# States kept at every second token, one scan for all tiles, and a decay product in four column quarters, in a two-block fp32 kernel

## The chip, the cores and the metric

The kernel runs on one core of a Trainium2 chip. The metric is the time of one execution on the device in microseconds (us). The engines are TensorE (PE; its weight loads are shown as PEld), VectorE (DVE), ScalarE (ACT), GpSimd (POOL) and SyncE (SP), which issues the loads of the weights.

## The reference

Two transformer-like blocks run one after the other on 256 tokens of width 2048, all in float32. The first has an attention, a gated linear attention (GLA) and a short convolution, the second has an attention with a window and an S5 state space, and each has a feed-forward part. Two places of it matter here.

The decay of the GLA goes through a product of rank 16:

```
z = (a_down @ gla_w_up[l]) + gla_b[l]          # a_down: 16 columns of h @ w_in
log_a = jax.nn.log_sigmoid(z) / GLA_GATE_TAU
```

The state space has 32 groups of 16 inputs and 64 complex states. Its states follow x[t] = A x[t-1] + B u[t], with A diagonal and complex, and its output is y = C x + D u:

```
bu_re = jnp.einsum('gph,blgh->blgp', bb_re, ug)
bu_im = jnp.einsum('gph,blgh->blgp', bb_im, ug)
...
_, _, xs_re, xs_im = lax.associative_scan(combine, (a_re_t, a_im_t, bu_re, bu_im), axis=1)
y = (jnp.einsum('ghp,blgp->blgh', c_re, xs_re)
     - jnp.einsum('ghp,blgp->blgh', c_im, xs_im)
     + d_skip.reshape(SSM_GROUPS, SSM_GROUP) * ug)
```

The output goes through an exact GELU and a gated linear unit (`w_glu`) into the second branch of the block.

## The kernel before

**Panels.** Every large product is cut into panels of 512 output columns for both tiles of 128 tokens. The weights come in chunks of four 128-row blocks, and each chunk is used in two pieces of two blocks (one or two blocks in the last chunks of the down projections). For each piece ScalarE writes the weights rounded to fp32r (`weights_hi`, L1202), VectorE writes the rest (`weights_lo`, L1772), and TensorE does three products for each row block and token tile: hi by hi (L584), lo by hi (L585), hi by lo (L586). A piece of two row blocks so has 12 panel matmuls. ScalarE and VectorE split three pieces ahead (`AHEAD = 3`), in a ring of four.

**Side work.** All else is written as generators, one of the same name for each engine. After each piece the engine's program takes one turn of its generator (`side.step()`), up to its next `yield`; in the panels of `q2` every fourth piece takes a second turn. A generator's end takes a turn as well. `side.finish()` runs what is left. Each engine works in its own program order; the engines meet at semaphores. Side work of TensorE (transposes at L608, products at other lines) thus stands between panel matmuls, and writes four PSUM banks called `side`. fp32 products appear in the trace as two records for each matmul call, transposes as one.

**The decay.** `a_down` splits `w_a_down` (16 columns) into hi and lo and multiplies it in three products for each of 16 row blocks, four row blocks to a turn (L761 to L763, 12 matmuls). Later `gla` multiplies the result by `w_up` (L842, 16 rows).

**The state space.** The states stand in 16 tiles of 128 (two groups each). `ssm_setup` runs beside the first panel of `down1`: VectorE works out A, the scaled B (`bb_re`, `bb_im`) and powers of A, TensorE transposes B. The matrices B and C have 32 rows or columns for each tile. After panel `u2`, `ssm_first_half` transposes u, and `ssm_input(0)` forms B u for the first eight tiles at all 256 tokens: for each tile one product of the real and one of the imaginary part in the row group of that tile (32 rows; L955, L956), four tiles to a turn. ScalarE copies them to `ssm_states` (L1552). `scan(0)` on GpSimd then goes over them: the 256 tokens are 16 blocks of 16; 15 steps inside all blocks at once, 15 carries from block to block, and then corrections of the tokens in each block by powers of A times the block's carry (L466, L468), three tiles at a time for six tiles. The other two tiles of the half are corrected by VectorE in `scan_end` (L2303, L2305), whose turns lie in those of the third of the attention's eight head pairs. `ssm_halves` follows them: `ssm_output(0)` multiplies by C (L973, L974: four tiles in four column quarters, two tiles' groups of `u` to the half), `ssm_input(1)` forms the second half, and `scan(1)` runs. Its output, `ssm_output(1)` in `ssm_end`, is taken beside the third panel of `branch_attn`, with VectorE's `scan_end(1)` beside the first two. The second half stands in the same memory as the first, so that it can't be formed before the first is used.

The waits at the place:

```
        pe.wait_ge(ev["scanned"], half + 1)
        pe.wait_ge(ev["scanned_dve"], half + 1)
        pe.wait_ge(ev["cT"], 2)
```

## Time and profile before

| | |
|---|---|
| median of 3 runs | 2915.58 us (2915.02 to 2915.74) |
| the profiled execution | 2915.55 us |
| its span, first to last instruction | 2914.3 us |
| TensorE's mean granted clock over the span | 0.997 of full |
| busy: PE, DVE, ACT, POOL | 2887.7, 1659.2, 1325.9, 284.7 us |
| data read from HBM | 532.55 MB, 183 GB/s over the span |

A row of the timeline has the start, the duration (of the merged run of instructions), engine, line, operation, output tile and inputs, shapes and count, and in brackets how long the engine was idle before it and what ended that. The drawn duration of a matmul is longer than the distance to the next one, since matmuls are pipelined: the distance between starts is what they cost. A wait is put down to the semaphore that came last.

### The profile page before, as it was taken

The page shows a single profiled execution, that of the slowest core. Times are in us where ns is not written, and L with a number is a line of the kernel's source. Part 1 is how long each engine was busy: PE and PEld are TensorE (multiplying, and loading weights), DVE is VectorE, ACT ScalarE, POOL GpSimd, SP SyncE. Part 2 cuts the span into 40 slices and gives each one's busy share as a digit, 9 for nine tenths or more (in the row PEclk, how much of TensorE's full clock was granted, in tenths as well). Part 3 has the DMA queues.
Part 4 walks back from the last instruction along what each step waited for, and adds up shares of the span by engine and source line. Part 5 has one row for each costly group of instructions (what it writes and reads, how often), then busy time and mean ns, then how long its engine had stood idle before and what let it go on. Part 6 is the DMA issues. An engine that isn't in the chain of part 4 may idle for free.

```text
span 2914.3 us, 32236 instructions
## 1 busy us (share of the span) xinstructions
PE 2887.7 (99%) x13280; PEld 2376.8 (82%) x13280; DVE 1659.2 (57%) x1874; ACT 1325.9 (45%) x1635; POOL 284.7 (10%) x369
## 2 busy tenths in 40 slices
PE   9999999999999999999999999999999999999998
PEld 7888887788888888888888888787788888888887
DVE  5464655555555554554574557667755666656444
ACT  5444445444444444444444455444544444444443
POOL 0000000000000000000000049795100000000000
PEclk9999999999999999999999999999999999999999
DMA  7545454555655566555655656454655555555563
GB/s 250 196 165 194 158 187 144 171 190 188 194 188 183 186 192 195 188 190 188 199 187 183 200 166 206 151 171 138 198 186 188 187 184 192 173 196 188 194 201 131
DMA packets 279295, 536.74 MB, mean 184 GB/s; under 512 B 17313, under 2 KB 20317, under 8 KB 279149
## 3 DMA queue, kind: packets, MB, share of 16 engines
q1 hardware_dynamic: 267520, 528.52, 55.4%
q10 hardware_dynamic: 11629, 6.17, 0.8%
q8 instruction: 105, 1.72, 0.2%
q14 instruction: 41, 0.34, 0.0%
HBM read 532.55 MB, written 2.10 MB: 183 GB/s over the span
## 4 chain that ended last, share of the span: by engine, by line
PE 93%; POOL 4%; DVE 1%; ACT 1%; issue 1%; DMA 0%; ACTq 0%; DVEq 0%; POOLq 0%
PE panels L584 30%; PE panels L586 29%; PE panels L585 29%; PE side L608 2%; POOL scan_step L442 1%; POOL ssm_states L447 1%; POOL scan_step L439 1%; POOL ssm_states L446 1%; POOL ssm_states L468 1%; POOL ssm_scratch L466 1%; DVE weights_lo L1772 0%; PE side L896 0%; PE side L597 0%; PE side L892 0%; PE side L881 0%
## 5 line engine op out<-in xcount | busy, mean ns | idle before, releaser
L1772 DVE TENSOR_TENSOR weights_lo<-weights,weights_hi 128x1024 fp32r<-128x1024 f32 (+1 forms) x1032 | 1258.2, 1225 | 1040.0 <-ACT weights_hi L1202 1034.6
L1202 ACT ACTIVATE weights_hi<-weights 128x1024 fp32r<-128x1024 f32 (+1 forms) x1032 | 1064.8, 1036 | 1140.0 <-PE panels L586 1121.9
L584 PE MATMUL panels<-weights_hi,xT_hi 128*128 128x512 f32 (+1 forms) x2752 | 1085.2, 394 | 0.9 <-DVE xT_lo L1820 0.8
L586 PE MATMUL panels<-weights_hi,xT_lo 128*128 128x512 f32 (+1 forms) x2752 | 1070.0, 389 | 0.0
L585 PE MATMUL panels<-weights_lo,xT_hi 128*128 128x512 f32 (+1 forms) x2752 | 1068.5, 388 | 0.0
L584 PEld LDWEIGHTS panels<-weights_hi,xT_hi 128*128 128x128 f32 x2752 | 517.4, 188 | 110.3 <-issue 7.4
L586 PEld LDWEIGHTS panels<-weights_hi,xT_lo 128*128 128x128 f32 x2752 | 516.9, 188 | 108.8
L585 PEld LDWEIGHTS panels<-weights_lo,xT_hi 128*128 128x128 f32 x2752 | 517.8, 188 | 101.7
L584 PE MATMUL panels<-weights_hi,hiddenT_hi 128*128 128x512 f32 x704 | 275.2, 391 | 0.0
L586 PE MATMUL panels<-weights_hi,hiddenT_lo 128*128 128x512 f32 x704 | 274.1, 389 | 0.0
L585 PE MATMUL panels<-weights_lo,hiddenT_hi 128*128 128x512 f32 x704 | 274.0, 389 | 0.0
L586 PEld LDWEIGHTS panels<-weights_hi,hiddenT_lo 128*128 128x128 f32 x704 | 132.1, 188 | 27.7
L585 PEld LDWEIGHTS panels<-weights_lo,hiddenT_hi 128*128 128x128 f32 x704 | 132.2, 188 | 27.3
L584 PEld LDWEIGHTS panels<-weights_hi,hiddenT_hi 128*128 128x128 f32 x704 | 132.2, 188 | 26.9
L398 POOL TENSOR_TENSOR rstd<-mean_squares,minus_half 128x2 f32<-128x2 f32 x5 | 3.5, 699 | 1286.5 <-DVE mean_squares L1835 1286.5
L398 POOL TENSOR_TENSOR rstd_first<-mean_squares,minus_half 128x2 f32<-128x2 f32 x1 | 0.7, 690 | 736.0 <-DVE mean_squares L1835 736.0
L442 POOL TENSOR_TENSOR scan_step<-ssm_states,ssm_vectors 128x128 f32<-128x128 f32 (+1 forms) x120 | 64.3, 559 | 0.0
L447 POOL TENSOR_TENSOR ssm_states<-ssm_states,scan_step 128x256 f32<-128x256 f32 (+1 forms) x60 | 52.0, 866 | 4.7
L584 PE MATMUL panels<-weights_hi,merged2T_hi 128*128 128x512 f32 x128 | 50.8, 397 | 0.0
L381 POOL TENSOR_TENSOR rstd_gla<-mean_squares,minus_half 128x2 f32<-128x2 f32 x4 | 2.8, 692 | 490.9 <-DVE mean_squares L2148 490.9
L584 PE MATMUL panels<-weights_hi,mixedT_hi 128*128 128x512 f32 x128 | 50.6, 395 | 0.0
L586 PE MATMUL panels<-weights_hi,merged2T_lo 128*128 128x512 f32 x128 | 50.0, 390 | 0.0
(323 smaller groups left out, 2090.4 us busy)
## 6 DMA issues: line engine op xcount, KB each, us to landing
weights<-in_w_in SPq DMA_DIRECT2D x162, 1024.0 KB, 5.0
weights<-in_w_up SPq DMA_DIRECT2D x88, 1024.0 KB, 5.0
weights<-in_w_ffn_gate SPq DMA_DIRECT2D x44, 1024.0 KB, 5.2
weights<-in_w_ffn_up SPq DMA_DIRECT2D x44, 1024.0 KB, 5.2
weights<-in_w_out SPq DMA_DIRECT2D x32, 1024.0 KB, 5.3
weights<-in_w_ffn_down SPq DMA_DIRECT2D x32, 1024.0 KB, 5.1
weights<-in_w_down SPq DMA_DIRECT2D x32, 1024.0 KB, 5.1
weights<-in_w_ffn_down SPq DMA_DIRECT2D x16, 768.0 KB, 4.4
```

Source lines behind the costliest of these rows:

```text
L439: pool.tensor_tensor(same, prev, row(0, 2), ALU.mult).then_inc(ev["pool_step"])
L442: pool.tensor_tensor(cross[:, c:c + 1], prev[:, 1 - c:2 - c], row(2 + c, 1), ALU.mult).then_inc(ev["pool_step"])
L446: step(pool.tensor_tensor(cur, cur, same, ALU.add))
L447: return pool.tensor_tensor(cur, cur, cross, ALU.add)
L466: step(pool.tensor_tensor(tmp, pr, last, ALU.mult))
L468: inst = pool.tensor_tensor(cur, cur, tmp, op)
L584: pe.matmul(acc, a, wh, start=k0 + k == 0, stop=False)
L585: pe.matmul(acc, a, wl, start=False, stop=False)
L586: inst = pe.matmul(acc, b, wh, start=False, stop=k0 + k == total - 1)
L608: return self.pe.transpose(out, in_, self.m.IDENT[0:in_.shape[0], 0:in_.shape[0]])
L1202: self.act.activation(self.m.HI[:, g % PIECES, 0:n], raw, ACT.Copy).then_inc(self.ev["hi_split"])
L1772: self.dve.tensor_tensor(m.LO[:, ring, 0:n], raw, m.HI[:, ring, 0:n].bitcast(F32), ALU.subtract).then_inc(self.ev["lo_split"])
```

## The change

The scan keeps only the state at the odd token of each pair. `ssm_input` forms AB u[2k] + B u[2k+1] in PSUM, for two state tiles to a bank, from two products with a moving operand that takes every second token, all 16 tiles at once right after `u2`. The scan works with A squared over 128 pairs: blocks of 8 pairs, 7 steps in two halves of the tiles that follow each other with scratch of their own, 15 carries over all tiles, corrections four tiles at a time. GpSimd does all of it, and VectorE's `scan_end` is gone. `ssm_output` (four turns behind the attention, in the last gate panel) takes the odd tokens as C x, and the even tokens as CA x[previous odd] + CB u[even], where CB (32x32 for each tile) and CA are made beforehand: CB by TensorE in `ssm_setup`, CA by VectorE in `ssm_input`. C is loaded and transposed in `ssm_setup` rather than after `u2`. The GELU follows in the same stage as the output.

In the decay, `w_a_down` stays fp32, padded with zeros to 32 columns, and each of four column quarters takes one of four row blocks, so that the result stands in four partial sums of 32 rows; `w_up` stands four times among zero rows and adds them up in the product with 128 rows.

Not in the cut below: names, memory offsets (`XS` holds 16 tiles of 128 pairs; `gate_bias_rows` moves), GpSimd's memset of `w_a_down` and VectorE's of `w_up`, four issues of the load of `w_up` instead of one, the coefficient rows that now hold A squared, VectorE's six products for CA, ScalarE's copies of CB and C, and the turns of ScalarE's GELU.

```diff
-    def scan(self, half):
+    def scan(self):
...
-        X5 = XS[:, :, :, :].rearrange("p c s (b j) -> p c s b j", j=BLK)
-        pool.wait_ge(ev["states_in"], nt * (half + 1))
+        X5 = m.XS[:, :, :, :].rearrange("p c s (b j) -> p c s b j", j=BLK2)
+        pool.wait_ge(ev["states_in"], nt)
...
             step(pool.tensor_tensor(cur, cur, same, ALU.add))
-            return pool.tensor_tensor(cur, cur, cross, ALU.add)
-
-        for j in range(BLK - 1):
-            step(advance(X5[:, :, :, :, j], X5[:, :, :, :, j + 1], 20, NB))
+            step(pool.tensor_tensor(cur, cur, cross, ALU.add))
+
+        for j in range(BLK2 - 1):
+            for half in range(2):
+                tiles = slice(half * nt, (half + 1) * nt)
+                advance(X5[:, :, tiles, :, j], X5[:, :, tiles, :, j + 1], m.STEP[:, half], 20, tiles, NB)
         for b in range(NB - 1):
-            inst = advance(X5[:, :, :, b:b + 1, BLK - 1], X5[:, :, :, b + 1:b + 2, BLK - 1], 24, 1)
-            if b < NB - 2:
-                step(inst)
-        inst.then_inc(ev["carried"])
-        pool.wait_ge(ev["carried"], half + 1)
-
-        nb, nj, ns = NB - 1, BLK - 1, 3
+            advance(X5[:, :, :, b:b + 1, BLK2 - 1], X5[:, :, :, b + 1:b + 2, BLK2 - 1], m.CARRY, 24, slice(0, ST), 1)
+
+        nb, nj, ns = NB - 1, BLK2 - 1, 4
         tmp = m.SCR[:, 0:ns * nb * nj].rearrange("p (s b j) -> p s b j", b=nb, j=nj)
-        for q in range(0, nt - SHARED, ns):
+        for q in range(0, ST, ns):
             for ci in range(2):
                 cur = X5[:, ci, q:q + ns, 1:NB, 0:nj]
                 for y in range(2):
-                    pr = m.POW[:, (ci + y) % 2, s0 + q:s0 + q + ns, 0:nj].unsqueeze(2).to_broadcast([P, ns, nb, nj])
-                    last = X5[:, y, q:q + ns, 0:nb, BLK - 1:BLK].to_broadcast([P, ns, nb, nj])
+                    pr = m.POW[:, (ci + y) % 2, q:q + ns, 1:2 * nj:2].unsqueeze(2).to_broadcast([P, ns, nb, nj])
+                    last = X5[:, y, q:q + ns, 0:nb, BLK2 - 1:BLK2].to_broadcast([P, ns, nb, nj])
                     step(pool.tensor_tensor(tmp, pr, last, ALU.mult))
                     op = ALU.subtract if (ci, y) == (0, 1) else ALU.add
                     inst = pool.tensor_tensor(cur, cur, tmp, op)
-                    if q + ns == nt - SHARED and (ci, y) == (1, 1):
+                    if q + ns == ST and (ci, y) == (1, 1):
                         inst.then_inc(ev["scanned"])
                     else:
                         step(inst)
...
 
         self.panel(plan.u2, X, side)
-        side.add(self.ssm_first_half(), self.ssm_outputs_setup())
+        side.add(self.ssm_input(), self.pause(3))
         for pan in plan.q2:
             self.panel(pan, X, side, dense=True)
         self.panel(plan.kv2, X, side)
-        side.add(self.attention2())
+        side.add(self.attention2(), self.ssm_output())
         for pan in plan.gate_attn + plan.gate_ssm:
             self.panel(pan, X, side)
         side.finish()
         pe.wait_ge(ev.attention[1]["outT_lo"], HEADS2 // 2)
         for p in range(3):
-            if p == 2:
-                side.add(self.ssm_end())
             self.panel(plan.branch_attn[p], (m.OH2, m.OL2), side)
         side.finish()
+        pe.wait_ge(ev["gel_lo"], 2)
         for pan in plan.glu:
             self.panel(pan, (m.GEH, m.GEL), side)
         side.add(self.glu_turned())
...
         yield
-        pe.wait_ge(ev["wad_lo"], 1)
-        ps = self.bank(0)[0:RANK, 0:S]
-        for k in range(KD):
-            pe.matmul(ps, m.WADH[:, k, :], m.XH[:, k, :], start=k == 0, stop=False)
-            pe.matmul(ps, m.WADL[:, k, :], m.XH[:, k, :], start=False, stop=False)
-            inst = pe.matmul(ps, m.WADH[:, k, :], m.XL[:, k, :], start=False, stop=k == KD - 1)
-            if k % 4 == 3 and k < KD - 1:
+        pe.wait_ge(ev["loaded_decay"], 16)
+        ps = self.bank(0)
+        for first in range(0, KD, 4):
+            for x in (m.XH, m.XL):
+                for g in range(4):
+                    k = first + g
+                    inst = pe.matmul(ps[32 * g:32 * g + 32, 0:S], m.WAD[:, k, :], x[:, k, :].bitcast(F32),
+                                     start=first == 0 and x is m.XH, stop=k >= KD - 4 and x is m.XL)
+            if first < KD - 4:
                 yield
...
+        pe.wait_ge(ev["bb_ready"], 4)
+        for b, src in enumerate((m.ABR, m.ABI)):
+            ps = self.bank(2 + b)
+            for u in range(4):
...
+            self.free(i, "cT", i + 1)
+        yield
+        pe.wait_ge(ev["cT"], 2)
+        ps = self.bank(0)
+        for u in range(4):
+            for bb, ct in ((m.BBR, m.CTR), (m.BBI, m.CTI)):
+                for j in range(4):
+                    s = 4 * u + j
+                    inst = pe.matmul(ps[32 * j:32 * j + 32, 32 * u:32 * u + 32], bb[:, s, :], ct[:, s, :],
+                                     start=bb is m.BBR, stop=bb is m.BBI)
+        inst.then_inc(ev["cb_done"])
+        self.free(0, "cb_ready", 1)
+        yield
...
-        pe.wait_ge(ev["bbT"], 2)
-        yield from self.ssm_input(0)
-
-    def ssm_input(self, half):
+        pe.wait_ge(ev["bbT"], 4)
+        for q in range(ST // 2):
+            ps = self.bank(q % 4)
+            for c, (ab, bb) in enumerate(((m.ABTR, m.BTR), (m.ABTI, m.BTI))):
+                for k in range(2):
+                    u, r = 2 * (q // 4) + k, slice(32 * (q % 4), 32 * (q % 4) + 32)
+                    o = (2 * c + k) * NK
+                    for w, bt in enumerate((ab, bb)):
+                        inst = pe.matmul(ps[:, o:o + NK], bt[r, u, :], m.UT[r, u, w:S:2], start=w == 0, stop=w == 1)
+            inst.then_inc(ev["bu_done"])
+            self.free(q % 4, "states_in", q + 1)
+            if q % 4 == 3:
+                yield
+
+    def ssm_output(self):
         pe, ev, m = self.pe, self.ev, self.m
-        nt = ST // 2
-        for s in range(nt):
-            ps = self.bank(s % 4)
-            u, r = (half * nt + s) // 4, slice(32 * (s % 4), 32 * (s % 4) + 32)
-            pe.matmul(ps[:, 0:S], m.BTR[r, u, :], m.UT[r, u, :], start=True, stop=True)
-            pe.matmul(ps[:, S:2 * S], m.BTI[r, u, :], m.UT[r, u, :], start=True, stop=True).then_inc(ev["bu_done"])
-            self.ssm_inputs += 1
-            self.free(s % 4, "states_in", self.ssm_inputs)
-            if s % 4 == 3:
-                yield
-
...
-        pe.wait_ge(ev["scanned"], half + 1)
-        pe.wait_ge(ev["scanned_dve"], half + 1)
-        pe.wait_ge(ev["cT"], 2)
-        for u in (2 * half, 2 * half + 1):
+        pe.wait_ge(ev["scanned"], 1)
+        pe.wait_ge(ev["cb_ready"], 1)
+        pe.wait_ge(ev["ca_ready"], 1)
+        for u in range(4):
             ps = self.bank(u)
-            for j in range(4):
-                o = ps[32 * j:32 * j + 32, 0:S]
-                s = 4 * u + j
-                x = s - half * ST // 2
-                pe.matmul(o, m.CTR[:, s, :], m.XS[:, 0, x, :], start=True, stop=False)
-                inst = pe.matmul(o, m.CTI[:, s, :], m.XS[:, 1, x, :], start=False, stop=True)
+            rows = [slice(32 * j, 32 * j + 32) for j in range(4)]
+            for c, ct in enumerate((m.CTR, m.CTI)):
+                for j, r in enumerate(rows):
+                    pe.matmul(ps[r, NK:S], ct[:, 4 * u + j, :], m.XS[:, c, 4 * u + j, :], start=c == 0, stop=c == 1)
+            for j, r in enumerate(rows):
+                pe.matmul(ps[r, 0:NK], m.CB[r, u, :], m.UT[r, u, 0:S:2], start=True, stop=False, skip_group_check=True)
+            for c, ca in enumerate((m.CAR, m.CAI)):
+                for j, r in enumerate(rows):
+                    inst = pe.matmul(ps[r, 1:NK], ca[:, 4 * u + j, :], m.XS[:, c, 4 * u + j, 0:NK - 1], start=False,
+                                     stop=c == 1, skip_group_check=True)
             inst.then_inc(ev["y_done"])
             self.free(u, "y_ready", u + 1)
             yield
-
...
+        for i, n in enumerate(("ssm_c_re_2", "ssm_c_im_2")):
+            for half in range(2):
+                act.dma_start(m.CRE[:, i, :, 64 * half:64 * half + 64],
+                              t[n][0].rearrange("(u r) h p -> (r h) u p", r=8)).then_inc(ev["loaded_c_proj"], 16)
...
+        for b, dst in enumerate((m.ABTR, m.ABTI)):
+            act.wait_ge(ev["bb_turned"], b + 3)
+            act.activation(dst[:, :, :], m.SIDE[:, 2 + b, :].rearrange("p (u s) -> p u s", u=4),
+                           ACT.Copy).then_inc(ev["bbT"])
+        yield
+        for q in range(ST // 2):
+            act.wait_ge(ev["bu_done"], q + 1)
+            s = 8 * (q // 4) + q % 4
+            act.activation(m.XS[:, :, s:s + 5:4, :],
+                           m.SIDE[:, q % 4, :].rearrange("p (c s t) -> p c s t", c=2, s=2),
                            ACT.Copy).then_inc(ev["states_in"])
-            if s % 4 == 3:
-                yield
...
         step(tt(ZI, V(T1), V(RD), ALU.mult))
         yield
-        step(dve.memset(m.BBR[:, :, :], 0.0))
-        step(dve.memset(m.BBI[:, :, :], 0.0))
+        for dst in (m.BBR, m.BBI, m.ABR, m.ABI):
+            step(dve.memset(dst[:, :, :], 0.0))
+        dve.memset(m.CTR[:, :, :], 0.0)
+        dve.memset(m.CTI[:, :, :], 0.0).then_inc(ev["c_zeroed"])
+        step(tt(T1, V(ABR), V(ZR), ALU.mult))
+        step(tt(T2, V(ABI), V(ZI), ALU.mult))
+        step(tt(AZR, V(T1), V(T2), ALU.subtract))
+        step(tt(T1, V(ABR), V(ZI), ALU.mult))
+        step(tt(T2, V(ABI), V(ZR), ALU.mult))
+        step(tt(AZI, V(T1), V(T2), ALU.add))
         dve.wait_ge(ev["loaded_b_proj"], 32)
         sc1 = m.TMP[:, 0:256].rearrange("p (s h) -> p s h", h=GROUP)
         sc2 = m.TMP[:, 256:512].rearrange("p (s h) -> p s h", h=GROUP)
...
+        zr, zi, azr, azi = (V(z).unsqueeze(2).to_broadcast([P, ST, GROUP]) for z in (ZR, ZI, AZR, AZI))
+        for n, (dst, x, y, op) in enumerate(((m.BBR, zr, zi, ALU.subtract), (m.BBI, zi, zr, ALU.add),
+                                             (m.ABR, azr, azi, ALU.subtract), (m.ABI, azi, azr, ALU.add))):
             step(dve.tensor_tensor(sc1, m.BRE[:, :, :], x, ALU.mult))
             step(dve.tensor_tensor(sc2, m.BIM[:, :, :], y, ALU.mult))
             for q in range(2):
...
-            yield
+        for u in range(4):
+            dve.wait_ge(ev["y_done"], u + 1)
+            y = m.UT[:, u, :].rearrange("p (k w) -> p w k", w=2)
+            dve.scalar_tensor_tensor(out=y, in0=y, scalar=m.V3[:, 14 + u:15 + u],
+                                     in1=m.SIDE[:, u, 0:S].rearrange("p (w k) -> p w k", w=2), op0=ALU.mult,
+                                     op1=ALU.add).then_inc(ev["y_ready"])
+            yield
+        low(0)
+        yield
         low(1)
 
     def attention2(self):
```

## Rows read from the trace of the kernel before

**Rows 1.** The page, part 1: busy time of each engine and share of the span.

```profile
PE 2887.7 (99%) x13280; PEld 2376.8 (82%) x13280; DVE 1659.2 (57%) x1874; ACT 1325.9 (45%) x1635; POOL 284.7 (10%) x369
```

**Rows 2.** The waits of TensorE: us in total, times, longest.

```profile
PE side L973 <- issue: 4.4, 2, 4.1
```

**Rows 3.** Timeline, TensorE at the three pauses.

```profile
1857.85 0.66 PE L608 MATMUL side<-identity,attn 128*128 128x128 f32 x2 [3.44 <-DVE attn L2384]
...
2003.14 0.50 PE L584 MATMUL panels<-weights_hi,attn2T_hi 128*128 128x512 f32 x1 [1.90 <-DVE weights_lo L1772]
...
2011.61 1.10 PE L973 MATMUL side<-ssm_states,cT_re 128*32 128x256 f32 x8 [4.14 <-issue]
```

**Rows 4.** Timeline, VectorE ahead of the first and the third pause.

```profile
1855.07 2.29 DVE L1772 TENSOR_TENSOR weights_lo<-weights,weights_hi 128x1024 fp32r<-128x1024 f32 x1
...
2010.88 0.63 DVE L2305 TENSOR_TENSOR ssm_states<-ssm_states,fix_scratch 128x450 f32<-128x450 f32 x1
```

**Rows 5.** Timeline of the setup beside `down1`: ScalarE, VectorE, TensorE.

```profile
1447.39 4.17 ACTq L1505 DMA_DIRECT2D b_im<-in_ssm_b_im  x1
...
1472.02 0.48 DVE L2213 MEMSET bb_re<- 128x512 f32 x1
...
1475.00 1.23 DVE L1772 TENSOR_TENSOR weights_lo<-weights,weights_hi 128x1024 fp32r<-128x1024 f32 x1
...
1479.25 0.39 PE L584 MATMUL panels<-weights_hi,hiddenT_hi 128*128 128x512 f32 x1
```

**Rows 6.** Windows: length, busy us of PE, PEld, DVE, ACT, POOL; granted clock.

```profile
1857.00:1862.00 5.00, 4.16 (x13) 3.44 (x14) 4.93 (x7) 1.33 (x2) 1.72 (x1) 0.66 0.62 208
2004.00:2008.00 4.00, 3.46 (x10) 2.16 (x8) 3.93 (x3) 1.35 (x3) 3.77 (x3) 0.57 0.00 0
2011.00:2015.00 4.00, 3.39 (x20) 2.03 (x21) 4.00 (x6) 0.00 (x0) 0.00 (x0) 0.57 0.20 79
```

**Rows 7.** Timeline of TensorE: side blocks between panel matmuls.

```profile
192.81 0.28 PE L761 MATMUL side<-xT_hi,w_a_down_hi 128*16 128x256 f32 x1
...
194.22 0.40 PE L584 MATMUL panels<-weights_hi,xT_hi 128*128 128x512 f32 x1
...
1707.13 1.03 PE L608 MATMUL side<-identity,projected 128*128 128x128 f32 x8
1707.92 0.48 PE L584 MATMUL panels<-weights_hi,xT_hi 128*128 128x512 f32 x1
...
1710.28 0.39 PE L585 MATMUL panels<-weights_lo,xT_hi 128*128 128x512 f32 x1
1710.51 0.39 PE L586 MATMUL panels<-weights_hi,xT_lo 128*128 128x512 f32 x1
1710.83 0.73 PE L955 MATMUL side<-uT,bbT_re 32*128 32x256 f32 x8
1711.36 0.63 PE L956 MATMUL side<-uT,bbT_im 32*128 32x256 f32 x8
1711.92 0.50 PE L584 MATMUL panels<-weights_hi,xT_hi 128*128 128x512 f32 x1
...
1847.21 0.39 PE L586 MATMUL panels<-weights_hi,xT_lo 128*128 128x512 f32 x1
...
1848.69 0.48 PE L584 MATMUL panels<-weights_hi,xT_hi 128*128 128x512 f32 x1
...
1866.43 0.39 PE L586 MATMUL panels<-weights_hi,xT_lo 128*128 128x512 f32 x1
...
1867.77 0.50 PE L584 MATMUL panels<-weights_hi,xT_hi 128*128 128x512 f32 x1
```

**Rows 8.** Instructions on the states: count, shortest, median, longest ns, first and last start.

```profile
L439 POOL TENSOR_TENSOR scan_step<-ssm_states,ssm_vectors x60: 227/764/1806, 1718.2 to 1975.1; 128x256 f32<-128x256 f32 x30, 128x16 f32<-128x16 f32 x30
...
L466 POOL TENSOR_TENSOR ssm_scratch<-a_powers,ssm_states x16: 1402/1960/2277, 1826.2 to 2006.3; 128x675 f32<-128x675 f32 x16
```

**Rows 9.** Windows again, columns as in rows 6: attention beside the scan.

```profile
1770.00:1850.00 80.00, 80.00 (x403) 64.80 (x402) 57.05 (x75) 38.47 (x70) 75.77 (x118) 1.00 0.58 192
```

More of the change, by code:

```diff
@@ L1146, in program @@
         self.panel(plan.u2, side)
-        for i, n in enumerate(("ssm_c_re_2", "ssm_c_im_2")):
-            for half in range(2):
-                act.dma_start(m.CRE[:, i, :, 64 * half:64 * half + 64],
-                              t[n][0].rearrange("(u r) h p -> (r h) u p", r=8)).then_inc(ev["loaded_c_proj"], 16)
         self.columns2(plan.u2, UCOL2)
-        side.add(self.ssm_first_half(), self.ssm_outputs_setup())
+        side.add(self.ssm_input(), self.pause(3))
         for p, pan in enumerate(plan.q2):
@@ L1722, in program @@
         side.finish()
-        side.add(self.pause(2), self.scan_end(1))
         for p in range(3):
-            if p == 2:
-                side.add(self.ssm_end())
             self.panel(plan.branch_attn[p], side)
```

219 lines of the change are left out of this document (82 added, 137 removed).

## The prediction

> **What bounds the kernel now.** I read the page first: TensorE is busy for 99% of the span [rows 1], so every matmul of the side work lies on the path that sets the end, and so does every pause. The list of waits on TensorE then says where it isn't busy [rows 2], and the timeline places three pauses in the state space's stretch: 3.44 us before 1857.85, 1.90 before 2003.14, 4.14 before 2011.61 [rows 3]. The first waits for VectorE to scale the attention's output, which comes behind a subtraction of the weights that takes 2.29 us there; the third ends when VectorE's own share of the state correction is done (2010.88 + 0.63) [rows 4]. That subtraction takes 1.23 us where GpSimd is idle [rows 5]. With the short wait at 1862 (the 4.4 of the list less 4.14) it is 9.7 us. Each pause also has a stretch beside it in which TensorE's clock is granted at its lower level, 1.2 instead of 2.4 GHz: 1.00 less the granted share, twice, times the window gives 3.4 us in each of the three windows [rows 6]. TensorE is at work for all of the first, some 2.8 us of the second and 3.2 us of the third, and loses half of that: 1.7 + 1.3 + 1.6 = 4.6. So 14.3 us hang on how the scan is done now. The rest of this forecast is what the change pays on TensorE for getting them.
>
> **Measure.** Panel matmuls start 0.23 us apart. A side block costs the time between the panel matmuls around it, less 0.23, plus 0.1 for the late second matmul behind it [rows 7].
>
> **What goes.** `scan_end` leaves VectorE, with both waits on `scanned_dve`. What would be late next is GpSimd's own scan. Before, one half took from 1718.2 to 1826.2 until its first correction pair, and a pair of 675 elements takes 2 x 1.96 us [rows 8]. The new scan has 14 block steps of the old size instead of 15, 15 carries of twice the width, and 16 correction pairs of 420 elements: about 105 us, then 16 times 2.5 to 3.9 us, so it ends between 1865 and 1890. TensorE asks for it in the last panel of the gates. There are 64 side turns in the eight gate panels; attention takes 58 and one to close, so the first output block has turn 60, near 1965. The slack is over 70 us, and I cost the wait at nothing; were it gone, each us would count in full. Subtractions against a working GpSimd remain until 1890, but they were there from 1770 to 1850 as well, with GpSimd busy for 75.77 of 80 us and TensorE for all 80 [rows 9]. I take the whole 14.3.
>
> A rule bears on this: the Trainium skill, "SBUF — State Buffer", "SBUF: two separate sides", has VectorE (with two inputs from SBUF) and GpSimd take one shared pair of ports exclusively for a whole instruction. The trace agrees: 2.29 against 1.23 us. By it shorter GpSimd instructions hold VectorE for less, which leaves the sum where it is.
>
> **`a_down`.** 12 matmuls with 16 columns of weights (192.81 to 194.22: 1.41 us) become 8 fp32 ones of 32 columns in four column quarters, two records each. That is the shape of the present output block: 1866.43 to 1867.77, less 0.23, plus 0.1 = 1.2 us [rows 7]. Four times 0.2 is 0.8 gained. The later product with `w_up` has 128 rows instead of 16 with the same columns: no more than a switch of shapes is gained, 0.1. The two small splittings of `w_a_down` on ScalarE and VectorE go, and a memset and three DMA issues come; those engines have subtractions in hand there, so nothing. Together -0.9 (-1.2 to -0.7 for a tenth each way on the blocks).
>
> **Setup on TensorE.** Eight more transposes for A·B: like the block at 1707.13, 0.9 us. C's transposes only move, from the q panels to `down1`: nothing. New is CB: 64 records of 32 columns, 16 in each column quarter. The nearest row is the 12 records of 64 columns from 1847.21 to 1848.69 (0.11 us each) [rows 7]; 16 such in parallel quarters make 1.8 plus the switch, half of that if the narrow record is cheaper: 1.2 to 2.0, I take 1.7. Sum +2.6.
>
> **Setup on the other engines.** VectorE's call that zeroes and fills `bb_re` now takes 1472.02 to 1475.00 [rows 5]. It gets four more memsets (0.48 plus a settle, 2.3 us), six products of 16 columns (0.2 each, 1.3) and then two more calls of 1.8. The call so ends 3.6 us later, at 1478.6, and the subtraction behind it at 1479.8; the panel piece that needs it began at 1479.25: 0.6 us late. The pieces after it take TensorE 2.7 us (12 matmuls) and more with the added transposes, VectorE 1.23 + 1.8: it keeps up. On ScalarE the four loads of C are issued right behind `b_im`, whose issue alone blocks the engine for 4.17 us [rows 5]. Behind it the splitting of weights waits, and VectorE for that. Bounds are 0 (they slip in) and another 4.5 us of blocking. The splitting runs three pieces of 2.7 us ahead, and 4.2 of those 8.1 are used already, so the upper bound gives a pause of about 1 there, and through VectorE up to 1 more at the late piece. CB waits for ScalarE's copies of C, some 0.4. I take 1.4 us in all, 0 to 3.5.
>
> **`ssm_input`.** Four blocks of 16 records (256 columns) become two of 64 records (128 columns). Now a block costs 1.3 us (1710.51 to 1711.92, less 0.23, plus 0.1), and in it all eight records of L955 start before the first of L956, although the code issues both for one tile before the next [rows 7]: four row groups work side by side, and records are taken out of program order across them. The new code gives 16 records running to one row group before it comes to the next. At 0.11 us each: all four groups side by side cost 1.8 + 0.4 a block, 4.4 in all against 5.3, -0.9; two at a time 4.0 a block, +2.6; one after another 7.6 a block, +9.8. The lookahead that the trace proves is 13 records: the fourth group's first stands behind 12 others. The new order needs 49 to have all four at work. I take two at a time and a little more, +2.8.
>
> A page speaks against this part: the Trainium skill, "TensorE: Matmul & The Clock Gate", "Step-by-step: what each phase is for", lets only weight loads be pulled ahead, while matmuls stay in program order; by it the sum would have +9.8 here. The trace of before does not agree, since L955 and L956 would alternate.
>
> **`ssm_output`.** Per u: in each quarter 4 records, then 2 of CB in 32x32 tiles, then 4, of 128 columns: 10 x 0.11 = 1.1, with four switches of tile shape and the 0.1 behind. The present block has 1.11 us between its panel matmuls less 0.23, of which four records of 256 columns are 0.88; the rest is two switches, 0.1 each. So 1.6 against 1.2. Four times 0.4 is +1.7. If CB's four small tiles can't write one bank at once, 0.66 more per u: +4.4. Reading every second token may cost too; no row shows it. I take +2.0 (+1.3 to +4.4).
>
> By the Trainium skill, "TensorEngine Tiling (Array Packing)", "Gotcha 1: PSUM Pressure", row tiles can't access one bank at the same time. No row of before has two of them in one bank; by it this term would be +4.4 and the time 2.4 us more.
>
> **VectorE's products of C with the decay** (six of 512 elements) come at about 1720, where the splitting is three pieces ahead and TensorE's pieces last longest: nothing; up to 1 if that cover is gone. ScalarE's state copies halve in number: off the path.
>
> **Sum.** -14.3 - 0.9 + 2.6 + 1.4 + 2.8 + 2.0 = -6.4. The profiled execution took 2915.55 us (its span 2914.3, 1.25 around it), 0.03 under the median of 2915.58, so I predict **2909.2 us**. All lower ends give 2902.5, all upper ends 2921.
>
> **Rivals.** What a measurement can't tell from no change is 0.2%, 5.8 us: 2909.75 to 2921.4.
> *Program order* (the other side): the row groups run one after another, +9.8 for +2.8: 2916.2, slower than before. It decides once the two input blocks cost over 14.5 us together. Against it stands the order of L955 and L956; for it, that no row shows a queue as deep as 16 in one group. The page named there says the same.
> *All side by side*: -0.9 for +2.8: 2905.5.
> *Setup takes over*: the queue behind `b_im` and the 7.2 us of VectorE's added work meet, a pause of over 3 us comes, and half a low-clock stretch with it: +5: 2914.
> *VectorE stays late*: the pauses come from GpSimd's hold on it more than from its own corrections. Half of the 14.3 stays: 2916. Against it: TensorE's 80.00 of 80 us under a busy GpSimd [rows 9].
> *Narrow tiles in one bank*: +2.4: 2911.6.
>
> **How the numbers follow.** My case 0.40, all side by side 0.20, program order 0.13, narrow tiles 0.12, setup 0.09, VectorE late 0.06. My case and the narrow tiles lie at the edge of what can be told; of the first six tenths are below 2909.75, of the tiles a quarter. Faster 0.48 (0.24 + 0.20 + 0.03 + 0.01), same 0.45, slower 0.07 (only several bad ends together pass 2921.4). The range 2903.5 to 2917.5 leaves under 2 in 10 out.
>
> **What would show it.** Right: no wait on VectorE's `attn` or on `ssm_states` in TensorE's list, the granted clock at full from 1850 to 2015, GpSimd done before 1890. For the input: two blocks, each with the gap between panel matmuls around it: 2.3 says side by side, 4 two at a time, 7.6 in order. For the output: gaps of 1.7 or 2.4. A pause of a panel matmul between 1450 and 1500 shows the setup's price. The prediction is wrong if a new low-clock stretch appears, or if the input's blocks leave 4 us far behind.

## The result, and the profile after

The changed kernel takes 2922.44 us, the median of 13 runs (2920.84 to 2926.93), against 2915.55 us for the kernel before in 13 runs beside them: ratio 1.0025, 95% interval 1.0017 to 1.0032. The interval leaves out 1: it is slower, by 6.9 us, where 6.4 less were forecast, and the time lies 5 us above the range. The profiled execution took 2920.84 us (span 2919.6); it is the fastest of the 13.

The page of the changed kernel, busy times, to set against [rows 1]: GpSimd does 107 us less, TensorE 12 us more.

```profile
PE 2899.9 (99%) x13528; PEld 2389.1 (82%) x13528; DVE 1639.2 (56%) x1880; ACT 1321.3 (45%) x1628; POOL 177.4 (6%) x215
```

Its list of TensorE's waits. The wait of [rows 2] for the states is gone, and so is the one for `attn` [rows 3]; a new one heads the list.

```profile
PE side L609 <- DVE log_dt_rows L2172: 1.8, 1, 1.8
...
PE panels L585 <- DVE weights_lo L1777: 0.6, 2, 0.5
PE side L852 <- DVE log_a L2115: 0.4, 1, 0.4
```

Its windows, of TensorE alone (length, busy us, granted clock, DMA share, GB/s). The stretches of [rows 6] at the lower level are gone: 1850 to 2015 is at full clock. Two others, of 6.8 us each, stand at the input's blocks, and TensorE is busy in every microsecond of them.

```profile
1710.00:1720.40 10.40, 10.40 (x79) 1.00 0.47 167
1720.40:1727.20 6.80, 6.80 (x28) 0.50 0.01 2
1727.30:1734.00 6.70, 6.70 (x64) 1.00 0.48 157
1734.10:1740.90 6.80, 6.80 (x20) 0.50 0.00 0
...
1850.00:2015.00 165.00, 165.00 (x933) 1.00 0.51 164
```

And the timeline of TensorE through the first input block, where [rows 7] has 1710.51 to 1711.92 for a block of before.

```profile
1715.35 0.39 PE L587 MATMUL panels<-weights_hi,xT_lo 128*128 128x512 f32 x1
1715.67 0.49 PE L975 MATMUL side<-uT,abT_re 32*128 32x128 f32 x2
...
1717.14 0.27 PE L975 MATMUL side<-uT,abT_im 32*128 32x128 f32 x1
1717.14 0.38 PE L975 MATMUL side<-uT,abT_re 32*128 32x128 f32 x1
...
1718.62 0.38 PE L975 MATMUL side<-uT,abT_re 32*128 32x128 f32 x1
...
1720.10 0.38 PE L975 MATMUL side<-uT,abT_re 32*128 32x128 f32 x1
...
1723.52 0.80 PE L585 MATMUL panels<-weights_hi,xT_hi 128*128 128x512 f32 x1
```

A row group's first product is `abT_re`. The second group's starts at 1717.14, beside the 13th of the first group's 16 records, with 3 more behind that one: 1.47 us after the first group's start at 1715.67, which is 13 times 0.113 us (12 records, of which the first counts double, since its second comes 0.22 us after it). The third and the fourth group start 1.48 us later each. So the groups run nearly one after another. The distance between the panel matmuls is 8.2 us here and 7.2 in the second block. Panel matmuls start 0.427 us apart at the lower level and 0.227 at the upper one, so each us at the lower level loses 0.47 us. With that taken out both distances are 6.7 us, and by the prediction's measure a block costs 6.6 us.

**Where the time went.** I compared the start of each piece of a panel in the two profiles. The changed kernel is 0.4 us ahead when the gated branch ends, 4.9 behind after the setup (C's transposes, moved there, are 0.9 of it and come back later), and 21.5 behind after the input (16.6 more, over two blocks where before had two short ones there and two later). Then it gains: the pauses and the two short later blocks fall away, the output's blocks cost 1.9 more, and it ends 5.3 us behind, which is the difference of the two spans.

### The profile page after: what moved, and what is told of

It reads as the page before. It is cut to its first block, busy times and chain, and to the rows that moved or that the text cites. A ratio compares the mean times of both kernels' runs of the same rounds, so it can differ in the third digit from the quotient of the medians.

```text
span 2919.6 us, 32575 instructions
## 1 busy us (share of the span) xinstructions
PE 2899.9 (99%) x13528; PEld 2389.1 (82%) x13528; DVE 1639.2 (56%) x1880; ACT 1321.3 (45%) x1628; POOL 177.4 (6%) x215
## 4 chain that ended last, share of the span: by engine, by line
PE 96%; DVE 2%; ACT 1%; issue 0%; ACTq 0%; DMA 0%; POOL 0%; DVEq 0%; POOLq 0%
PE panels L585 31%; PE panels L587 30%; PE panels L586 30%; PE side L609 3%; DVE weights_lo L1777 1%; PE side L975 1%; ACT weights_hi L1209 0%; PE side L899 0%; PE side L598 0%; ACTq L1512 0%; PE side L895 0%; PE side L884 0%; PE side L765 0%; PE side L1066 0%; PE side L1065 0%
## 5 line engine op out<-in xcount | busy, mean ns | idle before, releaser
L587 PE MATMUL panels<-weights_hi,mixedT_lo 128*128 128x512 f32 x128 | 49.9, 390 | 0.0
L586 PE MATMUL panels<-weights_lo,mixedT_hi 128*128 128x512 f32 x128 | 49.9, 389 | 0.0
L586 PE MATMUL panels<-weights_lo,merged2T_hi 128*128 128x512 f32 x128 | 49.8, 389 | 0.0
L1825 DVE SCALAR_TENSOR_TENSOR xT_lo<-side,vectors,xT_hi 128x256 fp32r<-128x256 f32 x64 | 27.7, 479 | 37.6 <-ACT xT_hi L1258 37.6
```

Source lines behind the costliest of these rows:

```text
L586: pe.matmul(acc, a, wl, start=False, stop=False)
L587: inst = pe.matmul(acc, b, wh, start=False, stop=k0 + k == total - 1)
L1825: inst = dve.scalar_tensor_tensor(out=lo[:, at + 2 * kp + k, :], in0=ps[:, k * S:(k + 1) * S], scalar=w, in1=hi[:, at + 2 * kp + k, :].bit ...
```

## The experiments

**1. Row groups innermost.** Why did the groups of the input's product run one after another? That is the first question.

```
-for q in range(8): for c, k, w: matmul(bank q % 4, row group q % 4)
+for half in range(2): for c, k, w: for j in range(4): matmul(bank j, row group j)
```

> The changed kernel with one edit: in a block of the input's product the row group is the innermost loop, so that four matmuls in a row go to four row groups and four banks; records, operands and sums stay. Theory (order of issue): the row groups of the changed kernel run one after another because 16 records in a row go to one group, and a group's first record starts only when some 3 records of the one before it are left. Then the gap between panel matmuls around a block falls from 6 to 7 us to about 2.3 us, the stretches of lower clock beside the blocks (1720.4 to 1727.3 and 1734.1 to 1740.9) go, and the time falls by 9 us of order and 6.8 us of clock, from 2922.4 to 2905 to 2908 us. Rival (the records themselves: pairs that add into one region, or the operand read at every second token, keep row groups apart): the gap stays over 5 us and the time within 2 us of 2922.

Measured: 2909.83 us (2907.76 to 2912.47, 11 runs), ratio to before 0.9979 (0.9970 to 0.9988): 12.6 us less than the changed kernel. The timeline of TensorE: eight records of four groups start together, and the block takes 1717.67 to 1720.02.

```profile
1717.67 0.39 PE L587 MATMUL panels<-weights_hi,xT_lo 128*128 128x512 f32 x1
1717.99 0.51 PE L977 MATMUL side<-uT,abT_re 32*128 32x128 f32 x8
1718.33 0.41 PE L977 MATMUL side<-uT,bbT_re 32*128 32x128 f32 x8
...
1720.02 0.50 PE L585 MATMUL panels<-weights_hi,xT_hi 128*128 128x512 f32 x1
```

No window at these blocks is below full clock. The order was the cause, and pairs and stride are no hindrance. The time is 2 us above the range that I expected, and its profile names two reasons: a stretch of 3.4 us at the lower level in the setup (behind the wait for `log_dt_rows`), and a new wait of 1.8 us for `weights_lo`. The second is VectorE, which in the three turns behind the input forms the products of C with the decay while GpSimd's scan has begun:

```profile
1728.12 1.44 DVE L1781 TENSOR_TENSOR weights_lo<-weights,weights_hi 128x1024 fp32r<-128x1024 f32 x1 [3.75 <-ACT weights_hi L1213]
1729.48 0.97 DVE L2287 TENSOR_TENSOR caT_re<-cT_re,ssm_vectors 128x512 f32<-128x512 f32 x1
1730.49 1.30 DVE L2288 TENSOR_TENSOR setup_scratch<-cT_im,ssm_vectors 128x512 f32<-128x512 f32 x1
...
1736.05 6.88 DVE L1781 TENSOR_TENSOR weights_lo<-weights,weights_hi 128x1024 fp32r<-128x1024 f32 x4
```

**2. Two groups at a time.** The same loop, with `j` over (0, 1) and then over (2, 3).

> As the first, but with two row groups interleaved at a time (groups 0 and 1, then 2 and 3). Theory (order of issue): two groups at work, a gap of about 3.7 us per block, 3 us less than in the changed kernel for each of the two blocks. Whether the lower clock comes is what this run is to tell: if it hangs on how much of the array is idle while no panel matmul runs, half the rows for 3.7 us may already escape it (2909 us); if it comes with any long block, 6.8 us more (2915 us). Rival (the records themselves): as the changed kernel, 2922 us.

Measured: 2910.38 us (2909.99 to 2912.20, 10 runs), gaps of 3.7 us, full clock at both blocks. Its two blocks take 2.9 us more than those of the first experiment, and its wait behind the input is 1.0 us instead of 1.8, so 2.1 us more are to be expected. The medians are only 0.5 apart, because the runs mix two cases: in both experiments the profile has a stretch of 3.4 us at the lower level in the setup, and some runs seem to escape it. The three runs of the first with a mean clock of 0.999 took 2907.8 to 2908.1 us, the six such runs of this one 2910.0 to 2910.5: 2.2 apart.

**3. Six microseconds, all rows at work.** What brings the lower clock: the length of the block, or how much of the array is at work in it?

```
 for half in range(2):
+    for again in range(3):
         for c, k, w: for j in range(4): matmul(bank j, row group j)
```

> The four row groups interleaved, and each block's matmuls issued three times over with the same operands and regions (the result stays the same): some 6.2 us a block with all four row groups at work, about as long as the changed kernel's blocks with one row group. Theory (the clock falls because three quarters of the array's rows are idle for those 6 us): the granted clock stays at its higher level, the gap is 5.5 to 6.5 us, the time 2913 to 2916 us. Rival (the clock falls because no panel matmul runs for that long): the two stretches of lower clock are there as in the changed kernel, 2920 to 2923 us.

Measured: 2917.46 us (2917.02 to 2919.42, 10 runs). The windows, of TensorE, over the two blocks of 5.9 us and behind them:

```profile
1712.00:1722.00 10.00, 10.00 (x174) 1.00 0.51 184
1722.00:1732.00 10.00, 10.00 (x264) 1.00 0.31 96
...
1742.00:1749.00 7.00, 5.13 (x16) 0.78 0.38 118
```

Full clock through both. Behind them one stretch of 3.4 us at the lower level lies between 1742 and 1749, at a wait of 1.9 us for `weights_lo` (another, as in experiments 1 and 2, is in the setup). In the changed kernel the lower level came 4.8 us after the first block's first record, and in experiment 5 below 3.3 us after it; here 5.9 us of side records pass without it. So length alone does not lower the clock when all four row groups work. The time is 1.5 us above my expectation, which had left out that wait and its clock.

**4. The same order, cut into four blocks.**

```
-            if q % 4 == 3:
+            if q % 2 == 1:
                 yield
```

> The changed kernel in its own program order, but with two row groups per side turn instead of four, so that the same matmuls come in four blocks of 32 records with a panel piece between them, and the pause of three turns behind them cut to one. Theory (order of issue, and the clock falls behind a long stretch of one busy row group): four gaps of about 3 us, so the 9 us of order stay, but the lower clock goes: 2915 to 2917 us. Rival (the clock is lost with the records in order however they are cut up): 2921 to 2924 us. A second rival is that VectorE, which waits for the last block before it forms the products of C with the decay, now comes late: a pause of up to 1 us in TensorE's list.

Measured: 2920.94 us (2917.92 to 2927.26, 11 runs). The edit did not do what was meant. In the panels of `q2` every fourth piece takes a second turn, and the third and fourth blocks fell into such a pair. The timeline of TensorE shows the second block alone, as the first is, and the last two with no panel matmul between them:

```profile
1722.30 0.39 PE L587 MATMUL panels<-weights_hi,xT_lo 128*128 128x512 f32 x1
...
1726.10 0.50 PE L585 MATMUL panels<-weights_hi,xT_hi 128*128 128x512 f32 x1
...
1728.72 0.39 PE L587 MATMUL panels<-weights_hi,xT_lo 128*128 128x512 f32 x1
...
1738.48 0.80 PE L585 MATMUL panels<-weights_hi,xT_hi 128*128 128x512 f32 x1
```

The two stretches at the lower level have become one of 10.2 us in the profile, which begins at 1731.9, in the third block. Its windows:

```profile
1727.00:1734.00 7.00, 7.00 (x51) 0.85 0.00 1
1734.00:1744.00 10.00, 10.00 (x42) 0.59 0.13 27
```

The two blocks that stood alone, 3.7 us each (3 us were expected) with 2.7 us of panel behind them, kept the full clock; it fell in the double block, which is as long as one of the changed kernel. So this run does not tell whether cutting protects the clock: four separate blocks were not run. That the time lies by the rival's 2921 says nothing for the rival. Single runs lie at 2918 and at 2927. The waits for VectorE are as in the changed kernel, so the second rival is out.

**5. C's loads later.** In the kernel before, ScalarE's splitting of the weights came right behind `b_im`, which ended at 1451.56 [rows 5]:

```profile
1451.61 2.01 ACT L1202 ACTIVATE weights_hi<-weights 128x1024 fp32r<-128x1024 f32 x2 [4.11 <-issue]
```

In the changed kernel C's four loads stand between them:

```profile
1446.98 3.96 ACTq L1512 DMA_DIRECT2D b_im<-in_ssm_b_im  x1
1450.97 1.66 ACTq L1516 DMA_DIRECT2D c_twice<-in_ssm_c_re  x2
1452.67 1.08 ACTq L1516 DMA_DIRECT2D c_twice<-in_ssm_c_im  x2
1453.80 2.96 ACT L1209 ACTIVATE weights_hi<-weights 128x1024 fp32r<-128x1024 f32 x3 [6.71 <-issue]
```

```
 sines of the setup
+for each of the four loads of C: yield; issue it
+yield; yield
```

> The changed kernel with one edit: ScalarE issues the four loads of C one per side turn behind its sines, not all at once behind b_im. Theory (the added issues are what holds the setup up): in the changed kernel the four issues take 2.74 us of ScalarE's queue behind b_im (1450.97 to 1453.75), the next splitting of weights starts at 1453.80 instead of 1451.61, VectorE gives log_dt_rows late and TensorE waits 1.8 us for it; in some profiles (the first three of the experiments) a stretch of lower clock of 3.4 us follows there, worth 1.7 us. With the loads later the wait for log_dt_rows goes, and the median falls by 1.8 to 3 us, to 2919.5 to 2920.6. Rival (VectorE's added memsets and products set the pause): the wait only moves to a later piece, and the time stays within 1 us of 2922.4.

Measured: 2921.03 us (2917.72 to 2922.55, 11 runs). The wait for `log_dt_rows` is gone and the piece around it takes 2.97 us instead of 4.80. The median fell by 1.4 only, and the intervals of the two ratios to the kernel before overlap (1.0008 to 1.0025, 1.0017 to 1.0032), so it is the profile that shows the gain, not the median. The input's order is unchanged, and in this profile the two stretches at the lower level are 10.2 us each instead of 6.8.

```profile
1717.20:1727.30 10.10, 10.10 (x45) 0.50 0.05 5
...
1730.90:1740.80 9.90, 9.90 (x46) 0.50 0.00 0
```

**6. Runs of 8 records.** Between the changed kernel's runs of 16 and the first experiment's of 2.

```
 for half in range(2):
+    for i in (0, 4):
+        for j in range(4): four of the eight (c, k, w) from i on, row group j
```

> The changed kernel, with four matmuls (8 records) in a row to one row group before the next group's four, twice round; the changed kernel has runs of 16 records, the first experiment runs of 2. Theory (a row group's first record starts once some 3 records of the one before it are left, and nothing further down the queue is looked at): each change of group costs 5 records of 0.113 us, so a block takes 7 changes x 5 + 8 = 43 records, 4.9 us, and the gap around it is 5.2 us. Rival (the queue reaches deeper, so that a group whose run is short is overtaken by the next two): 2.3 to 3.7 us. Whether the lower clock follows: by the theory that it hangs on idle rows, a block with little more than one group at work for 4.9 us may bring it, 2917 to 2920 us with it and 2914 to 2915 us without.

Measured: 2916.05 us (2912.96 to 2917.69, 10 runs). The timeline of TensorE: the second group starts 0.57 us after the first, beside the fifth of its eight records; the gap from 1717.90 to 1723.30, less 0.23 and plus 0.1, is 5.3 us (5.2 expected).

```profile
1717.90 0.39 PE L587 MATMUL panels<-weights_hi,xT_lo 128*128 128x512 f32 x1
1718.22 0.49 PE L976 MATMUL side<-uT,abT_re 32*128 32x128 f32 x2
1718.56 0.38 PE L976 MATMUL side<-uT,bbT_re 32*128 32x128 f32 x2
1718.78 0.50 PE L976 MATMUL side<-uT,abT_re 32*128 32x128 f32 x4
...
1723.30 0.58 PE L585 MATMUL panels<-weights_hi,xT_hi 128*128 128x512 f32 x1
```

One stretch of 3.4 us at the lower level stands behind the first block, and one in the setup. The time is between my two figures, and the runs are spread over both.

**7. All three edits.** The first, the fifth, and VectorE's products moved to six turns of the attention, one each, after GpSimd's scan.

```
+ca = Side(self.ssm_ca())      # the six products, a yield behind each
 for p in range(-1, PAIRS):
     for n ...:
+        if p in (5, 6) and n >= 3:
+            ca.step()
         yield
```

> The changed kernel with three edits: the input's row groups interleaved (first experiment), C's loads later (fifth), and VectorE's six products of C with the decay moved from the three turns behind the input, where they took 6.5 us beside a working GpSimd and left TensorE waiting 1.8 us, to six turns of the attention after GpSimd's scan. If the three costs are separate: 2909.8 - 1.8 (setup's wait) - 1.7 (its lower clock) - 1.9 (the products) = 2904.4 us. Rival (in the later turns the products find VectorE as loaded, and the wait comes back there): 2906 us with a wait for weights_lo between 1930 and 1960.

Measured: 2904.32 us (2904.14 to 2906.55, 5 runs), ratio to before 0.9961 (0.9949 to 0.9974). The three costs add up: 5.5 us less than the first experiment, where 5.4 were expected. The only wait left for `weights_lo`, 0.5 us, is in the setup, so the rival is out. Its page, and the first of the moved products on VectorE, 0.68 us where it took 0.97 beside the scan in the first experiment:

```profile
PE 2884.5 (99%) x13528; PEld 2374.9 (82%) x13528; DVE 1640.7 (57%) x1880; ACT 1320.7 (45%) x1628; POOL 175.5 (6%) x215
```

```profile
1912.23 0.68 DVE L2289 TENSOR_TENSOR caT_re<-cT_re,ssm_vectors 128x512 f32<-128x512 f32 x1
```

Between the first matmuls and the last 8 us the granted clock never falls.

**8. The kernel before without VectorE's share of the correction.** Were the pauses of [rows 3] VectorE's doing?

```
 for ci, y in scan_end of each half:
-    tmp = powers * last; state = state +- tmp
+    on the first only: copy one column of the state onto itself
```

> The kernel before, without VectorE's share of the state correction: the two tiles of each half that VectorE corrects stay uncorrected, and one copy of one column stands in for the eight instructions of each half; all waits, queues and the order of work stay. Theory of the prediction (all three pauses and the clock beside them hang on how the scan is done): the first pause (3.44 us before 1857.85, VectorE late with the attention's output) and the third (4.14 us before 2011.61) go, and with them 1.7 and 1.6 us of lower clock; of the second (1.90) it says nothing sure. So 2915.6 - 10.9 = 2904.7 us, or 2901.5 if the second goes too. Rival (VectorE is late because GpSimd holds it): the first pause stays and only the third goes: about 2910 us. A second rival is that TensorE then waits for GpSimd's own correction, which in the trace of before ends only little ahead of VectorE's: 2907 to 2909 us.

Measured: 2911.91 us (2911.13 to 2913.44, 10 runs). The first pause and the one of 1.90 us go, but TensorE's list has a new head:

```profile
PE side L973 <- POOL ssm_states L468: 8.2, 2, 6.2
```

The second rival's mechanism held, 3 us above its figure: in the profile of before GpSimd's last correction ended 1.2 us ahead of VectorE's. The waits moved on to it, with 10.2 us at the lower level beside them, as much as before. So unloading VectorE alone gives 4 us; the rest of the gain takes the shorter scan.

**9 and 10. The length of a run, in the kernel before.** Both issue each of its input's products twice; only the order differs.

```
 9:  for each tile: (B_re, B_im) x 2                    runs of 8 records
 10: for again in range(2): for each of 4 tiles: (B_re, B_im)   runs of 4
```

> The kernel before, with each of its input's products issued twice into the same region (the result stays the same), the second time right behind the first: runs of 8 records of 256 columns in one row group instead of 4. There are no accumulating pairs and no reading of every second token here, so only the length of the run differs from a kernel known to run side by side. Theory (the next row group starts when some 3 records of the one before are left): three changes of group at 5 records each and 8 for the last, 23 records of 0.22 us, a gap of 5.3 us in place of 1.3 in each of four blocks: +16 us, and a stretch or two of lower clock beside them (1.7 us each): 2932 to 2936 us. Rival (what kept the changed kernel's groups apart was its pairs or its stride): four groups side by side, 8 records each, a gap of 2.2 us, 2919 to 2920 us.

> The kernel before with the same doubled work as the ninth experiment, in the other order: all four tiles of a block once, then all four again, so that runs stay at 4 records. Theory: the groups stay side by side, 32 records in four groups, a gap of 2.2 us (0.9 more than before) in each of four blocks: 2919 to 2920 us, and no new stretch of lower clock. Rival (each change of group costs, whatever the order): as much as the ninth or more.

Measured: 2929.40 us (2928.43 to 2931.98, 4 runs) and 2920.00 us (2919.45 to 2920.67, 10 runs): 9.4 us apart for the same matmuls. The ninth's gaps are 5.03 us where the clock is full (5.3 expected), the tenth's 2.25 (2.2). The timelines of TensorE in the ninth and in the tenth:

```profile
1710.94 0.69 PE L956 MATMUL side<-uT,bbT_re 32*128 32x256 f32 x2
1711.48 0.59 PE L957 MATMUL side<-uT,bbT_im 32*128 32x256 f32 x2
1711.91 0.70 PE L956 MATMUL side<-uT,bbT_re 32*128 32x256 f32 x4
...
1715.78 0.50 PE L584 MATMUL panels<-weights_hi,xT_hi 128*128 128x512 f32 x1
```

```profile
1711.66 0.73 PE L957 MATMUL side<-uT,bbT_re 32*128 32x256 f32 x8
1712.20 0.63 PE L958 MATMUL side<-uT,bbT_im 32*128 32x256 f32 x8
...
1713.72 0.50 PE L584 MATMUL panels<-weights_hi,xT_hi 128*128 128x512 f32 x1
```

In the ninth the second group starts 0.97 us after the first, beside its fifth record; in the tenth all four groups' first records start within 0.04 us. The ninth came out 3 us under its range. Three of its four blocks stayed at full clock; a stretch of 6.8 us at the lower level began in the third. The later blocks also took something off the pauses that follow: 2.8 us for `attn` and 2.7 for the states, where before had 3.4 and 4.1.

**11. Without the CB product in the output's blocks.**

```
-matmul(quarter j, columns 0..127, CB[row group j], uT even)        x4
+matmul(quarter j, column 0, cT_re, one state)                      x4
```

> The seventh experiment's kernel without the product of CB with the inputs in the output's blocks (the even tokens lack that part; one matmul of one column per quarter stands in for the four 32x32 ones). Theory (the four narrow tiles work side by side in one bank, as their starts 7 ns apart in the trace of the changed kernel say): each of the four gaps falls from 1.6 us by less than 0.3 us, the time by 0.5 to 1.2 us. Rival of the prediction (the narrow tiles cannot write one bank at once): each gap falls by 0.9 us, the time by 3.5 us.

Measured: 2902.33 us (2902.28 to 2903.01, 4 runs), 2.0 less than the seventh; each of the four gaps falls by 0.43 us (1.7 in all), between the two theories' figures. The timeline of the changed kernel shows the narrow records of the four quarters starting together, 7 ns apart, and the time that they hold is two records one behind the other (0.22 us) and the changes of shape on both sides:

```profile
1983.69 0.40 PE L991 MATMUL side<-ssm_states,cT_im 128*32 128x128 f32 x8
1984.03 0.43 PE L993 MATMUL side<-uT,cb 32*32 32x128 f32 x8
1984.38 0.42 PE L996 MATMUL side<-ssm_states,caT_re 128*32 128x127 f32 x8
```

## Why the prediction was wrong

**The step that failed is `ssm_input`**, "I take two at a time and a little more, +2.8". Two blocks of 6.6 us against four of 1.28 are +8.1. I had the answer in the rival *program order* and gave it 0.13. Its +9.8 is too much by 1.0 a block, because the last 3 records of each group overlap the next group. My ground against it was that before's records of L955 and L956 are out of program order across groups, from which I read a lookahead of 13 records, as if it reached over any records. With such a reach the second group's first record would have started when the first group still had some 12 of its 16 to do; it started with 3 left. Experiments 6, 9 and 10 and the two kernels show a rule that gives the picture of before as well: the next group's first record starts beside the fourth-last record of the run ahead of it. In a run of 4 that is the first one, so nobody is held up: in the kernel before, the four groups' first records start 13 ns apart (1710.83 to 1710.87). A run of 8 holds the next group up by 0.57 us (0.97 with 256 columns), a run of 16 by 1.48. It fits the gaps of 5.3 and 6.6 us in the changed kernel and its variants and those of 1.28, 2.25 and 5.03 us in the kernel before and its variants. So the order of L955 and L956 showed no deep lookahead, and it was no ground against the rival: records start out of program order across groups, but only from the last four of a run on. What in the engine sets that number is not shown.

**A term was missing: the clock behind the input.** Two stretches of 6.8 us at the lower level took 0.47 of 13.7 us, +6.4. The prediction named "a new low-clock stretch" as what would make it wrong, but had no price for it beside the input; only the rival on the setup had half a stretch. *Program order* with the 6.4 gives 2922.6, next to the 2922.4 measured, but partly by luck: its input term is 1.7 too high, and the setup's stalls are 1.0 too low. That the order decides about these stretches is shown (experiment 1 has none there), and so is that length alone does not bring them (experiment 3). Experiment 2 adds nothing on this, since in experiment 4 blocks of the same 3.7 us kept the full clock in program order too. For blocks in between it is open: of those of 5 us in experiments 6 and 9 some had a stretch and some had none.

**Right.** The 14.3 us of the scan stage: no wait for `attn` or for the states, full clock from 1850 to 2015, and GpSimd's last correction starts at 1894.2 (its end was forecast for 1890 at the latest; but the scan began at 1735.8, 17.6 us later than before's, and its length was as forecast), over 70 us before it is asked for. By the distances between starts, which are what matmuls cost, the stage had held up TensorE for 10.5 us of pauses and 4.3 of clock, so 14.8. The rival *VectorE stays late* is out. `ssm_output`: the gap is 1.69 us against 1.21, four times 0.48 = +1.9 (+2.0 forecast), and *narrow tiles in one bank* is out: they start together. Setup on TensorE: A·B's transposes 0.9, CB 0.9 (1.7 forecast: the narrow records start 0.06 us apart in groups of eight, about half the price), so +1.8 for +2.6. The late piece on VectorE is 0.6, as forecast.

**Off in size.** The issues behind `b_im` cost a pause of 1.8 us, where the upper bound had about 1 and the sum 0.8 for all but the late piece; so the setup's stalls are +2.4 instead of +1.4. `a_down` gained 0.15 a block instead of 0.2, and with `w_up`'s neighbours 0.4 instead of 0.9 in all. VectorE's products of C cost nothing in the changed kernel, as forecast, but only because the slow input covered them: with it mended they cost 1.8 us, where I had said "up to 1 if that cover is gone".

**The sum again**, by what was measured: -14.8 - 0.4 + 1.8 + 2.4 + 8.1 + 6.4 + 1.9 = +5.4; the two profiles differ by 5.3. For the seventh experiment: -14.8 - 0.4 + 1.8 + 0.6 - 0.7 (two blocks of 2.2) + 1.9 = -11.6; the medians differ by 11.6 and the profiles by 11.0. Of the other 1.6 us between +5.3 and the medians' +6.9, longer stretches at the lower level are the likely cause: the two slowest runs, 2926 and 2927 us, have a mean clock of 0.994. The rest have 0.996 or 0.997, as the profiled one, which is too coarse to tell. What decides the length in a run is open.

## What to carry to other kernels

Where matmuls use a part of TensorE's rows each, the order of issue decides whether they work side by side: put the row group in the innermost loop, one bank each, and keep runs in one group to four records or fewer (four held nobody up, eight did; five to seven were not run). Read the start times of the first record of each group, not the engine's busy time, which was 100% while most of the time three quarters of the rows were idle. Price the clock too where a block keeps one row group at work for long (blocks of 5 to 7 us here), and when a slow block is mended, look at what it had been covering.

## What the runs showed that I had not expected

- The next row group starts beside the fourth-last record of the run ahead of it: the 13th of 16 (1.47 us later), the fifth of 8 (0.57 us later), the first of 4 (13 ns later).
- TensorE at work in every microsecond got the lower clock level for 6.8 us twice (and 10.2 us twice in experiment 5) during and behind work with one row group of four at a time; with four groups at work for 5.9 us it did not. Blocks of 3.7 us kept the full clock, with two groups at work (experiment 2) as with one (the first two of experiment 4).
- A side turn is not always followed by a panel piece: where a piece takes two turns, two blocks become one, and experiment 4 lost its question by that.
- Four small DMA issues on ScalarE's queue, 2.74 us of issue behind a load whose own issue took 3.96 us, became 1.8 us of TensorE's time, because the splitting of weights and VectorE's step were queued behind them.
